# A three-tap convolution's passes spread over attention steps, its last product behind a gate unit, and the values split per head

## The reference, cut to what matters

```python
h = rms_norm(x, norm_mix_pre)
q, k, v, cb, cc, cx, g_att, g_conv = split(h @ w_in)
# 8 heads of 64; strictly causal, in blocks of 128 queries
z = q @ k.T / 8
w = exp(log_sigmoid(z) + later)      # later: sum of log_sigmoid(-z) over keys between s and t
o = w @ v
y_att  = o @ w_att_branch
y_conv = (cb * causal_dwconv(cc * cx, conv_mix_w)) @ w_conv_branch
merged = sigmoid(g_att) * y_att + sigmoid(g_conv) * y_conv
```

## Time and profile before

| | us |
|---|---|
| median of 3 runs (2276.4 to 2278.12) | 2277.32 |
| the profiled execution, its own time | 2277.11 |
| its span | 2275.1 |
| mixed stage, from / to, in the span | 752 / 1320 |
| TensorE busy in the span | 2138.6 (94%) |
| TensorE busy in the mixed stage | 536.0 of 568 |
| VectorE, ScalarE, GpSimd busy in the mixed stage | 351.6, 275.5, 149.3 |

### The profile page before, as it was taken

How to read it: one execution, slowest core, us unless ns; L and a number is a source line. 1 busy time by engine, 2 the same in 40 slices (tenths; PEclk the granted TensorE clock), 3 DMA queues, 4 the chain that set the end, 5 groups by cost and what they waited for, 6 DMA issues and landing times.

```text
span 2275.1 us, 27632 instructions
## 1 busy us (share of the span) xinstructions
PE 2138.6 (94%) x10609; PEld 1769.5 (78%) x10609; DVE 1136.8 (50%) x1547; ACT 831.4 (37%) x1477; POOL 673.5 (30%) x527
## 2 busy tenths in 40 slices
PE   6898998999998999898998999989999999999996
PEld 4686878999776778687877888868888888878785
DVE  7357656989435276675656654263222222221523
ACT  5133216888323254463645532242122112111212
POOL 3222140000022422132221245223333333367672
PEclk8999999999999999999999999999999999999998
DMA  5031121010132211121212254231111111132432
GB/s 168 29 122 38 56 75 44 10 48 10 51 115 80 65 54 55 42 69 33 83 46 79 99 168 157 86 107 49 46 46 51 51 46 46 46 105 98 139 111 74
DMA packets 142919, 164.65 MB, mean 72 GB/s; under 512 B 7091, under 2 KB 108999, under 8 KB 142823
## 3 DMA queue, kind: packets, MB, share of 16 engines
q1 hardware_dynamic: 118663, 98.10, 14.1%
q10 hardware_dynamic: 24160, 65.23, 8.2%
HBM read 133.94 MB, written 29.36 MB: 72 GB/s over the span
## 4 chain that ended last, share of the span: by engine, by line
PE 84%; DVE 10%; ACT 3%; issue 2%; DMA 1%; ACTq 0%; DVEq 0%
PE psum L589 18%; PE psum L591 18%; PE psum L590 17%; PE psum L886 15%; PE psum L798 3%; PE psum L809 3%; PE psum L824 1%; PE psum L825 1%; PE psum L826 1%; PE psum L923 1%; PE psum L907 1%; DVE softplus_part L1994 1%; PE psum L599 1%; PE psum L940 1%; PE psum L908 1%
## 5 line engine op out<-in xcount | busy, mean ns | idle before, releaser
L534 POOL TENSOR_TENSOR w_ring<-w_staging,zero 128x8 fp32r<-128x8 f32 x172 | 47.3, 275 | 1548.6 <-PE psum L591 1055.3
L537 POOL TENSOR_TENSOR w_ring<-w_staging,w_ring 128x1024 fp32r<-128x1024 f32 (+1 forms) x172 | 440.3, 2560 | 14.4
L886 PE MATMUL psum<-h,w_ring 128*128 128x512 f32 x1728 | 440.8, 406 | 0.7 <-ACT v L1380 0.7
L886 PEld LDWEIGHTS psum<-h,w_ring 128*128 128x128 f32 x1728 | 322.3, 193 | 69.3 <-ACT v L1380 1.1
L589 PE MATMUL psum<-ffn_in,w_ring 128*128 128x512 f32 x672 | 265.4, 395 | 0.0
L591 PE MATMUL psum<-ffn_in,w_ring 128*128 128x512 f32 x672 | 264.2, 393 | 0.0
L590 PE MATMUL psum<-ffn_in,w_ring 128*128 128x512 f32 x672 | 263.8, 393 | 0.0
L2116 DVE SCALAR_TENSOR_TENSOR up_buf<-psum,vectors,up_buf 128x1023 f32<-128x1023 f32 x44 | 56.4, 1283 | 308.3 <-ACT up_buf L1598 308.3
L535 POOL TENSOR_SCALAR w_ring<-w_staging 128x1016 fp32r<-128x1016 f32 (+1 forms) x172 | 183.0, 1064 | 0.0
L591 PEld LDWEIGHTS psum<-ffn_in,w_ring 128*128 128x128 f32 x672 | 126.0, 188 | 30.5
L590 PEld LDWEIGHTS psum<-ffn_in,w_ring 128*128 128x128 f32 x672 | 126.3, 188 | 29.3
(11 more groups left out here) (273 smaller groups left out, 4494.0 us busy)
## 6 DMA issues: line engine op xcount, KB each, us to landing
w_staging<-in_w_in SPq DMA_DIRECT2D x58, 512.0 KB, 3.8
w_staging<-in_w_up SPq DMA_DIRECT2D x44, 512.0 KB, 3.8
w_staging<-in_w_down SPq DMA_DIRECT2D x44, 512.0 KB, 3.2
w_staging<-in_w_out SPq DMA_DIRECT2D x16, 512.0 KB, 3.8
scratch_gates<-gate_out ACTq DMA_DIRECT2D x32, 256.0 KB, 2.4
merge_gates<-scratch_gates ACTq DMA_DIRECT2D x16, 512.0 KB, 4.5
x_again<-scratch_x ACTq DMA_DIRECT2D x16, 512.0 KB, 4.3
xin<-in_x ACTq DMA_DIRECT2D x8, 512.0 KB, 3.2
```

The lines of the kernel that those rows point to most:

```text
L537: pool.tensor_tensor(lo[:, 0:width], WS[:, s, 0:width], plain(hi[:, 0:width]), ALU.subtract).then_inc(S["w_split"], 1)
L886: ins = pe.matmul(mix_bank(h), (sl if x == 2 else sh)[:, P * k:P * k + P], ml if x == 1 else mh, start=m == 0, stop=m == UNIT // 2 - 1)
```

## The change

The order of units `BESIDE` gets a gate unit between cx and cb of each of the four conv blocks, taken from the gates that stood behind it. `evacuate` of a cx half keeps the product alone; its three taps become `conv_pass`, one per step, at the end of VectorE's step. The passes of half 0 begin in the step in which the half of cx is done, those of half 1 when cx is done and half 0's are through. The last product now waits for a counter of passes (six per block). The values are split per head instead of per pair: for the next pair's first head in steps 10, 26 and 42, for its second head in steps 22, 38 and 54; the waits of TensorE and of the SP queue are counted accordingly. Places of the halves, by the planner:

| block | cx half 0, 1 | last product before | last product after | passes of half 0 | of half 1 |
|---|---|---|---|---|---|
| 0 | 0, 1 | 3, 4 | 5, 6 | 0 to 2 | 3 to 5 |
| 1 | 15, 17 | 18, 19 | 21, 22 | 15 to 17 | 18 to 20 |
| 2 | 31, 32 | 34, 35 | 36, 37 | 31 to 33 | 34 to 36 |
| 3 | 47, 49 | 50, 51 | 53, 54 | 47 to 49 | 50 to 52 |

```diff
-BESIDE = (CONVS[0][1:] + GATES[0:3] + CONVS[1][:1] + CONVS[1][1:] + GATES[3:6] + CONVS[2][:1]
-          + CONVS[2][1:] + GATES[6:10] + CONVS[3][:1] + CONVS[3][1:] + GATES[10:])
+BESIDE = (CONVS[0][1:2] + GATES[0:1] + CONVS[0][2:] + GATES[1:3] + CONVS[1][:1]
+          + CONVS[1][1:2] + GATES[3:4] + CONVS[1][2:] + GATES[4:6] + CONVS[2][:1]
+          + CONVS[2][1:2] + GATES[6:7] + CONVS[2][2:] + GATES[7:10] + CONVS[3][:1]
+          + CONVS[3][1:2] + GATES[10:11] + CONVS[3][2:] + GATES[11:])
+def conv_passes():
+    out = {}
+    for f in range(4):
+        step = 0
+        for h in range(2):
+            place = min(p for p, of in DONE.items() if (MIX.index(("cx", f)), h) in of)
+            step = max(step, place[0])
+            for tap in range(3):
+                out[step] = (f, h, tap)
+                step += 1
+    return out
...
-                    sp.wait_ge(S["vh_set"], 4)
-                    sp.wait_ge(S["vh_hi"], 4)
+                    sp.wait_ge(S["vh_set"], HEADS)
+                    sp.wait_ge(S["vh_hi"], HEADS)
...
-                if p % 8 == 0:
-                    pe.wait_ge(S["vh_set"], p // 8 + 1)
+                if p % 4 == 0:
+                    pe.wait_ge(S["vh_set"], h + 1)
...
-            def values_hi(pair_of_heads):
+            def values_hi(pair_of_heads, x):
                 if pair_of_heads:
-                    act.wait_ge(S["av2_mm"], 8 * pair_of_heads)
-                cols = slice(P * pair_of_heads, P * pair_of_heads + P)
-                act.activation(VH[:, :, :, 0, :], VR[:, :, cols].rearrange("p t (h d) -> p t h d", d=DH), ACT.Copy).then_inc(S["vh_hi"], 1)
+                    act.wait_ge(S["av2_mm"], 8 * pair_of_heads - 4 + 4 * x)
+                first = P * pair_of_heads + DH * x
+                act.activation(VH[:, :, x, 0, :], VR[:, :, first:first + DH], ACT.Copy).then_inc(S["vh_hi"], 1)
...
-                if i > 1 and i % (2 * TT) == 1:
-                    values_hi(i // (2 * TT))
+                if i % (2 * TT) == 10 and i // (2 * TT) < 3:
+                    values_hi(i // (2 * TT) + 1, 0)
+                elif i % (2 * TT) == 6 and i > 2 * TT:
+                    values_hi(i // (2 * TT), 1)
...
                         v.tensor_tensor(prod, mix_bank(h), prod, ALU.mult).then_inc(S["mix_v"], 1)
-                        v.wait_ge(S["mix_v"], 4 * f + h + 1)
-                        if f and h == 0:
-                            v.wait_ge(S["cv_st"], 16 * f)
-                        shifted = lambda d: PROD[:, 2 - d + FW * h:2 - d + FW * h + FW]
-                        link(v.tensor_scalar(CY[:, cols], shifted(0), VEC[:, 2, nf + f:nf + f + 1], None, ALU.mult))
-                        link(v.scalar_tensor_tensor(out=CY[:, cols], in0=shifted(1), scalar=VEC[:, 1, nf + f:nf + f + 1],
-                                                    in1=CY[:, cols], op0=ALU.mult, op1=ALU.add))
-                        v.scalar_tensor_tensor(out=CY[:, cols], in0=shifted(2), scalar=VEC[:, 0, nf + f:nf + f + 1],
-                                               in1=CY[:, cols], op0=ALU.mult, op1=ALU.add).then_inc(S["cv_y"], 1)
                     elif kind == "cb":
                         mix_ready(v, u, h)
-                        v.wait_ge(S["cv_y"], 2 * f + h + 1)
+                        v.wait_ge(S["cv_y"], 6 * f + 3 * h + 3)
                         v.tensor_tensor(CY[:, cols], mix_bank(h), CY[:, cols], ALU.mult).then_inc(S["mix_v"], 1)
+            def conv_pass(f, h, tap):
+                cols = slice(FW * h, FW * h + FW)
+                taken = PROD[:, 2 - tap + FW * h:2 - tap + FW * h + FW]
+                weight = VEC[:, 2 - tap, nf + f:nf + f + 1]
+                if tap == 0:
+                    v.wait_ge(S["mix_v"], 4 * f + h + 1)
+                    if f and h == 0:
+                        v.wait_ge(S["cv_st"], 16 * f)
+                    v.tensor_scalar(CY[:, cols], taken, weight, None, ALU.mult).then_inc(S["cv_y"], 1)
+                else:
+                    v.wait_ge(S["cv_y"], 6 * f + 3 * h + tap)
+                    v.scalar_tensor_tensor(out=CY[:, cols], in0=taken, scalar=weight, in1=CY[:, cols],
+                                           op0=ALU.mult, op1=ALU.add).then_inc(S["cv_y"], 1)
...
                 evacuate((i, 2))
-                if i > 1 and i % (2 * TT) == 1:
-                    values_lo(i // (2 * TT))
+                if i in PASSES:
+                    conv_pass(*PASSES[i])
+                if i % (2 * TT) == 10 and i // (2 * TT) < 3:
+                    values_lo(i // (2 * TT) + 1, 0)
+                elif i % (2 * TT) == 6 and i > 2 * TT:
+                    values_lo(i // (2 * TT), 1)
```

More of the change, by code:

```diff
@@ L191 @@
 DONE = beside_done()
+def conv_passes():
[9 more added lines that the diff above has]
+    return out
+PASSES = conv_passes()
 def tm_signals():
@@ L1456, in evacuate @@
                         if f and h == 0:
-                            act.wait_ge(S["cv_y"], 2 * f)
+                            act.wait_ge(S["cv_y"], 6 * f)
                         mix_ready(act, u, h)
@@ L1496, in _ @@
             act.wait_ge(S["tm_free"], T_OUT2)
-            values_hi(0)
+            values_hi(0, 0)
+            values_hi(0, 1)
             evacuate((-1, 2))
@@ L1962, in _, with values_lo @@
                                            op0=ALU.mult, op1=ALU.mult).then_inc(S["x1_out"], 1)
[L1963 to L1968, removed]
+            def values_lo(pair_of_heads, x):
+                first = P * pair_of_heads + DH * x
+                v.wait_ge(S["vh_hi"], 2 * pair_of_heads + x + 1)
+                v.tensor_tensor(VH[:, :, x, 1, :], VR[:, :, first:first + DH], plain(VH[:, :, x, 0, :]),
+                                ALU.subtract).then_inc(S["vh_set"], 1)
             def stack_lo(u, h):
@@ L2031, in evacuate @@
                         v.tensor_tensor(prod, mix_bank(h), prod, ALU.mult).then_inc(S["mix_v"], 1)
-                        v.wait_ge(S["mix_v"], 4 * f + h + 1)
-                        if f and h == 0:
-                            v.wait_ge(S["cv_st"], 16 * f)
-                        shifted = lambda d: PROD[:, 2 - d + FW * h:2 - d + FW * h + FW]
-                        link(v.tensor_scalar(CY[:, cols], shifted(0), VEC[:, 2, nf + f:nf + f + 1], None, ALU.mult))
-                        link(v.scalar_tensor_tensor(out=CY[:, cols], in0=shifted(1), scalar=VEC[:, 1, nf + f:nf + f + 1],
-                                                    in1=CY[:, cols], op0=ALU.mult, op1=ALU.add))
-                        v.scalar_tensor_tensor(out=CY[:, cols], in0=shifted(2), scalar=VEC[:, 0, nf + f:nf + f + 1],
-                                               in1=CY[:, cols], op0=ALU.mult, op1=ALU.add).then_inc(S["cv_y"], 1)
                     elif kind == "cb":
                         mix_ready(v, u, h)
-                        v.wait_ge(S["cv_y"], 2 * f + h + 1)
+                        v.wait_ge(S["cv_y"], 6 * f + 3 * h + 3)
                         v.tensor_tensor(CY[:, cols], mix_bank(h), CY[:, cols], ALU.mult).then_inc(S["mix_v"], 1)
+            def conv_pass(f, h, tap):
[11 more added lines that the diff above has]
+                                           op0=ALU.mult, op1=ALU.add).then_inc(S["cv_y"], 1)
             v.memset(ONE[:, :], 1.0).then_inc(S["ones_set"], 1)
             v.memset(PROD[:, 0:2], 0.0).then_inc(S["cv_pad"], 1)
-            values_lo(0)
+            values_lo(0, 0)
+            values_lo(0, 1)
             v.wait_ge(S["ones_set"], 1)
```

## The result

The changed kernel takes 2257.05 us (median of 4, 2254.08 to 2258.98) against 2276.86 (4, 2275.61 to 2278.12) of the kernel before: a ratio of 0.9913, 95% interval 0.9900 to 0.9925, so 17 to 23 us faster. Forecast were 2247.7 us and 29.65 us of gain, with a range of 2241 to 2260. The time lies in the wide range but outside the forecast's own one (2243 to 2252), and a third of the forecast gain is missing.

The account below looks back on a forecast made before the run. Bound: TensorE's waits in the mixed stage (32 us idle, 27.7 of them on VectorE's exponent) and clock falls behind them. 4.7 + 6.75 + 1.8 + 1.55 + 4.9 + 10.45 - 0.5 = 29.65 us off gives 2247.7 us, range 2241 to 2260.

Parts of the forecast that it names:

- rival B: Clock falls all the same behind short waits, so all 10.45 us of clock gain are lost: 2258 us, chance 0.1.
- E: Slower: moved work in wide steps lies uncovered on the path exponent, weights_lo, transposes: 2296 us, chance 0.03.
- The three first waits: Borders 1 to 3: two passes leave the front of the exponent, each wait shrinks by 1.57 us, 4.7 us in all.
- Second waits of borders 1 and 3: Less VectorE work ahead of the exponent takes 3.3 us off border 1 and 3.45 off border 3, 6.75 in all.
- Start and second wait of border 2: One pass replaces three, but the scan then waits for GpSimd's subtract: 1.8 us gained at the start, 1.55 at border 2.
- the open point: Whether a pass between GpSimd's two instructions delays the subtract: the row said no, the lock rule yes, 0.4 us each place.
- Third waits: Borders 1 and 3: exponent's 640 column scan starts ahead of GpSimd's subtract, saving 4.9 us.
- rival A: 640 column scans at steps 20 and 52 still wait for the subtract: gain 23.2 us, 2254 us, chance 0.2.
- The clock: Clock falls vanish where waits over 1.7 us shrink under 0.9: 4.8, 1.65 and 4.0 us at borders 1 to 3, 10.45.
- Step 6: A pass in step 5 delays weights_lo by 0.78 us against 0.32 slack: 0.46 us new TensorE wait, cost 0.5.
- Values per head: Eight half-width conversions, VectorE's about 0.7 us each, were taken as covered by its idle time: cost 0.
- The fall at the start: At the start about 2 us of wait stay, so the clock's fall behind it, 1.8 us from 800 to 816, stays too.

Follow-up runs that it names:

- experiment 3: Changed kernel with the values made per pair at the border as before, so the convolution's part alone: 2253.56 us, ratio 0.9891 to the kernel before.
- experiment 2: Changed kernel without the pass in steps 1 and 32, right behind the unit whose end lets GpSimd split: 2252.07 us, ratio 0.9882 to the kernel before.
- experiment 7: Kernel before with only the new order of units `BESIDE`, passes and values as before: 2273.19 us, ratio 0.9979.
- experiment 5: Changed kernel with ScalarE's high half of the values one step earlier, VectorE's low half unmoved: 2243.19 us, ratio 0.9844 to the kernel before.
- experiments 1: Changed kernel with VectorE's low half of the values one step later, ScalarE's high half unmoved: 2251.58 us, ratio 0.9884 to the kernel before.
- 8: Changed kernel measured once more, nothing altered: 2256.53 us, ratio 0.9905 to the kernel before.
- experiment 4: Kernel before with only the values split per head, passes and order of units as before: 2286.20 us, ratio 1.0034.
- experiment 6: Changed kernel with ScalarE's high half one step earlier and no pass in steps 1 and 32: 2241.19 us, ratio 0.9837 to the kernel before.

## Why the prediction was right, and where it was off

The time fell into the range of 2241 to 2260 us, but one step of the working failed, and by a sign of the prediction's own: it would be wrong if TensorE got new waits in steps 21 to 24, and it got one of 2.39 us in step 23. That the time is in the range all the same is luck as far as this step goes: the range reached up to 2260 for rival B's sake, and no rival had this mechanism. E came nearest, with the path exponent, `weights_lo`, transposes, but for the moved work's own length and the lock, not for a wait for ScalarE. Term by term:

- **The three first waits** (forecast 0.64, 0.2, 0.66 left): 0.64, 0.19, 0.66. Right.
- **Second waits of borders 1 and 3** (0.7, 0.85 left): 0.55, 0.82. Right, and experiment 3 shows the values' share: with them 2.21 and 2.45.
- **Start and second wait of border 2** (2.2, 1.7 left): 2.28 and 2.22. The lock did move from the pass to the scan, as forecast. On the open point, whether a pass that slips in pushes the subtract back, the answer is that it does: the pass overlaps the subtract's start at 800.22 by 0.45 us (it ends at 800.67), and the subtract lasts 2.68 us instead of 2.43. The Trainium skill (SBUF — State Buffer, Who interferes with whom) says that the engine that comes second stands until the other's instruction is done. The trace agrees, though the stretch is 0.25 us and not the whole 0.45. In the earlier trace rows the overlap was 0.2 us and left no mark, and this is the same pattern: wherever a pass or a scan was under way when a subtract started, the subtract lasted longer by the overlap less about 0.2 us (0.45 gave 0.25, 0.82 gave 0.6 in experiment 2, 1.25 gave 1.0 at 937.08, 2.05 gave 1.8 at 1093.01). The row I took as speaking against the rule was too short an overlap to show it.
- **Third waits** (0.45 to 0.5 left): 0.33, 0.55. The scans of 640 columns took 1.79 and 2.00 us, in front of the subtract; rival A did not come. Experiment 7 has this term alone.
- **The clock** (10.45): no fall behind a wait under 0.9 us in any profile here, so the step holds and rival B is out. Experiment 5 gives the size: of its 30.4 us of stage the waits on the exponent and on `weights_lo` make 19.2, which leaves 11.2, with 1.7 of them for the fall at the start that didn't come; 9.5 against 10.45. The reading behind it was too regular. I said that matmuls run slower behind each such wait, some 1.75 us for each. Behind the third wait of border 3 (3.00 us, 1226.64) there is no fall in the kernel before: the granted clock is 1.00 in every slice from 1216 to 1240. What the clock lost at that border (5.1 us by slices of 4 us) belongs to two waits, 1.7 behind 2.23 and 3.4 behind 4.30.
- **Step 6** (0.46 us): 0.21. The waits of 0.22 and 0.23 in other steps stand in the kernel before too (0.22, 0.24, 0.20).
- **Values per head is the step that failed.** It reads: "In step 23 VectorE stands idle for 1.72 us ahead of the low half at 978.94, which covers what step 22 gets". I priced VectorE's 0.7 us, compared it with slack on the same engine, and put the cost at nothing. I left out what the instruction waits for: the high half of ScalarE, put behind `soft_part(i+2)` of the same step. The wait is 3.91 us, not 0, TensorE sees 6.9 us of it at the three second heads, and behind two of the three a fall of the clock (granted 0.68 and 0.90 in the two stretches of 4 us from 1096 on, 0.89 and 0.68 in those from 1224 on, so 1.7 us each): together 10.3 us, and experiment 5 gives back 10.2 of stage. The first heads' waits, 1.92 or 1.93 us each in steps 10, 26 and 42, are under narrower exponents, and TensorE has no wait for `weights_lo` of 0.15 us or more between them and the next border. Half the information was in the earlier trace rows: the values' low half was among the instructions ahead of the border's exponent, and at border 2 of the kernel before it already stood for ScalarE's high half, 2.68 us long:

```profile
1070.37 1.22 DVE L1967 TENSOR_TENSOR v_split<-v,v_split 128x1024 fp32r<-128x1024 f32 x1 [2.68 <-ACT v_split L1405]
```

Each of the other waits came within 0.55 us of its forecast, and this one term was 10 us off: 29.65 against 20.2 us. The fall at the start, which was to stay and didn't come in the first profile, hid 1.7 us of that. The chance for the forecast's own range (2243 to 2252) was too high at 0.55; the time fell beyond it, towards B, for another reason than B's. Still open is a remainder of a few microseconds that differs from one execution to the next (below).

## What to carry to other kernels

When an instruction is moved, price the wait of its producer in the new place, not its duration: what stands in the other engine's queue ahead of what it needs. A two-engine handover (high half here, low half there) should have its halves in different steps, the producer's first. Moving the consumer a step later helped too, but cost 2.8 us of new waits here. Work that an engine does right behind the event that starts a rival on a shared resource met that rival in every profile in which it stood there, so order it such that the critical instruction gets there first and let the engine with time to spare be the one that stands.

## What the runs showed of the hardware that was not expected

- Whether the granted clock falls behind a wait of about 2 us is a matter of the single execution, as the changed kernel's two profiles show. Behind the same wait of 2.28 to 2.29 us at the start, with the same instructions around it, it fell in experiments 1 and 8 and not in the changed kernel's first profile, 3 and 5; behind 2.40 us in step 23 it fell in 2 and 4 and not in the changed kernel and 8. Longer waits of about 3 us don't settle it either: no fall behind 3.00 us at 1226.64 in the kernel before, one behind 3.00 us at 1230.71 in experiment 4 and none behind 3.06 at 1072.55. Behind 4.0 to 4.3 us it fell all seven times, in four of them for 3.4 us of lost time instead of the usual 1.7 (at 1209.31 in the kernel before and three times in experiment 7); behind under 0.9 us never. In experiment 6, whose profile has no wait over 0.9 us and no fall in this stage, five runs still spread over 6.6 us; what varies there is open.
- Between VectorE and GpSimd either one can be the one that stands, and it shows as duration, not as a later start: a subtract of 2.4 us lasted 3.46 at 937.08 in the changed kernel behind the scan of 640 columns, and 3.01 in experiment 2. The first 0.2 us of overlap left no mark, 0.2 us at 802.04 in the kernel before for one; why isn't shown.
